# Retention of prompt tiles 3 to 5 moved from the phases before the gathers into the second group's front

## The chip, the cores and the metric

One of the eight cores of a Trainium2 chip runs the whole program. The metric is the device time of one execution in microseconds. The kernel before ran three times: 3722.57, 3725.55 and 3727.93 us, median 3725.55 us.

## The reference

One layer works on 1024 prompt tokens (8 tiles of 128) and 128 sample tokens (one tile, number 8), width 1024, float32 throughout.

```
h = rms_norm(x);  z = h @ w_in         # split into rq rk rv rg (retention), fq fk fv (attention), ff
retention:  rotary on rq, rk; state recurrence over the tiles; output o = intra part + q @ state
            state' = state * decay + k^T v      (tile t needs the state after tile t-1)
attention:  QK-normed, with a cumulative forget bias, causal over all earlier tiles
x = x + concat(rms(o) * silu(rg), rms(attention)) @ w_out
x = x + peer(rms_norm(x)):  q = x @ wq; scores against 2 x 128 keys per head, top 16 of each side,
            16 best of the sums -> 128 experts per token (8 heads x 16);
            y += sum over the 128 experts of softmax * gelu(x . u[e]) * v[e]
```

Every token takes 128 rows of the table `peer_uv` (u and v side by side, 8 KB each). That is 1152 gathers of 128 rows, 1208 MB, for nine tiles.

## The kernel before, in words

**Phases ahead of the tail.** Four programs run one after the other with a barrier between (line 105): `phase_norm` (normed rows turned into `hT`, and the RQ projection), `projection([RK, RV])`, `phase_retention` (recurrence, gate projection RG, gated output stored to `rets`; the sample's new state in four pieces, one in each of four steps; the loads and stores on SP), and `projection([FQ, FK, FV])` for tiles 0 to 2. The list `EARLY` says which tiles the retention half does here: all but `AFTER = [6, 7]`, so tiles 0 to 5 and 8. In all these phases the normed rows of tiles 3 to 8 are also stored to the scratch `hts`, and the pair state after tile 5 to `bds`.

**The tail.** `phase_tail` has two kinds of work on the same engines. The *strips*: for each tile 128 gathers by POOL (L1842) into a ring of nine buffers, a dot product of each on DVE (L2748), four at a time weighed into a strip (L2757 to L2770, with a tanh on ACT, L2055), and added on PE (L2391), which frees four buffers. There are 32 strips to a tile. The *front*: attention, output projection, query projection, scores and top-k choice of the tiles that come later, in three groups of three tiles. A choice ends with ACT moving 16 blocks of indices (L1894); tile t's first gathers wait for those moves. So group 1's front has to be done when tile 2's gathers run out, and group 2's when tile 5's do.

**What sets the order.** `front_steps` lists the front's steps with what each needs, `deal` places every step of every engine between two units of strip work (gather, dot, strip) by a table of assumed costs, and the engines then run these fixed lists. A step that finds no place while there is still strip work is put ahead of the next tile's first unit. Within an engine nothing overtakes.

**Steps in the diff and the prediction.** Group 1's front is, in order: `pmm` and the like (FQ, FK, FV of tiles 3 to 8), `decay`/`foxs`/`foxp`/`foxv` (attention), `hturn`/`hmm` (output projection), `rq` (query projection, L2339: 4 blocks x 3 tiles), `rturn` (L2348), `rscore` (L2357), `rtop` (L2441 to L2454), `rcand` (the choice, L2467 to L2539), `rexp` and `rmove` (the index and gate moves). `retain` lists the retention of late tiles: `lload` (weights, 2 MB each), `lhts` (normed rows, rotary tables, pair state), `lmm` (a projection of a tile, L2159), `lrot`/`lcat` (rotary, L2598 to L2607), `lturn`, `lsc`, `lout`, `lup`. Before the change `retain` is called for group 2 alone. The `rcand` of tile 3 needs the last `rscore` of group 1.

Of the kernel before, what the change touches and what calls it, by code (L numbers as in the profile page):

```python
# [32 lines left out]
def emit(nc, a):  # L33

    ctx = ExitStack()
    with ctx:
# [83 lines left out]
        AFTER = [6, 7]  # L120
# [478 lines left out]
        def phase_retention(block, sem, ps):  # L599
# [3 lines left out]
            PIECE = {ORDER[2 + r]: r for r in range(PAIRS)}  # L603
# [35 lines left out]
            def _(sp):  # L639
# [7 lines left out]
                for s, t in enumerate(ORDER):  # L647
                    sp.wait_ge(rg_done, s + 1)
                    sp.dma_start(a["rets"][t], mixo[:, t, 0:GW]).then_inc(out_done, 16)
                    if t in PIECE:  # L650
                        r = PIECE[t]
# [13 lines left out]
            def _(pe):  # L665
# [100 lines left out]
                for s, t in enumerate(ORDER):  # L766
# [14 lines left out]
                    if t in PIECE:  # L781
                        state_sample(PIECE[t])
                    for k in range(LEAD if t == ST else 0 if whole else KC - 1, KC):
                        gate(t, k)
                    if t == ST:
                        turn_sample()
# [14 lines left out]
            def _(dve):  # L801
# [66 lines left out]
                for s, t in enumerate(ORDER):  # L868
                    if s + 1 < STEPS:
                        mask(ORDER[s + 1])  # L870
                    if t < PT:
                        state(t)
                    if t in PIECE:
                        add_state(PIECE[t])
                    if s + 1 < STEPS and ORDER[s + 1] in PIECE:
                        spread(PIECE[ORDER[s + 1]])
                    gated(t)

# [54 lines left out]
        LATE, NL = TILES - GT, len(AFTER)  # L933
# [6 lines left out]
        def front_steps():  # L940
# [49 lines left out]
            def retain(g, routed):  # L990

                n, NJ = 4 * GT, 4 * NL
                add(rest, ("lload", g, 0), sp=(bulk((2.1, 16)), ("pe", ("rq", g - 1, 2 * GT - 1, 1))))
                add(rest, ("lload", g, 1), sp=(bulk((2.1, 16)), ("pe", ("rq", g - 1, 3 * GT - 1, 1))))
                add(rest, ("lhts", g), sp=(bulk((0.52 * NL, 4), (0.1, 0.25), (0.26, 2)), ("pe", ("rq", g - 1, n - 1, 1))))
                for j in range(NJ + 1):
# [16 lines left out]
                    elif m >= 3 * NL:  # L1013
                        add(rest, ("lgate", g, m), act=(0.7, ("pe", ("lmm", g, m, 1))),
                            dve=(2.0, ("act", ("lgate", g, m)), ("pe", ("lmm", g, NJ - 1, 1))))
# [63 lines left out]
            for g in range(GROUPS):  # L1079
                lo, hi, nt = FIRST[g], FIRST[g + 1], len(tiles_of(g))  # L1080
                routed = [("pe", ("rscore", g - 1, 4 * GT - 1))] if g else []
                if g == 1:
                    project(routed + [("dve", ("rtop", 0, 4 * GT - 1, 4))])
                    routed = [("sp", ("pact", 0, PJ - 1)), ("sp", ("pturn", 0, 2 * LATE - 1)), ("sp", ("pnrm", 0, 2 * LATE - 1))]
                if nt < GT:
                    retain(g, routed)
                    routed = [("dve", ("lret", g, NL - 1)), ("dve", ("lup", g, NL - 1))]
# [19 lines left out]
                if g:  # L1107
                    at = routed if nt < GT else [("sp", ("pturn", 0, 2 * LATE - 1)), ("pe", ("pmm", 0, 2 * LATE - 1, 1))]
                    add(rest, ("loadk", g), sp=(bulk((0.26 * (GT * g + nt), 4)), *at))
# [264 lines left out]
        def phase_tail(block, sem, ps):  # L1374
# [33 lines left out]
            def wq(g, b):  # L1408
# [23 lines left out]
                   for i in range(LATE)]  # L1432
# [5 lines left out]
            NL = len(AFTER)  # L1438
            l_h = [M[:, 35840 + D * i:35840 + D * (i + 1)].rearrange("p (k n) -> p k n", k=KC) for i in range(NL)]
            l_rot = [M[:, 34304 + GW * i:34304 + GW * (i + 1)] for i in range(3)]  # L1440
            l_q = [M[:, 37888 + GW * i:37888 + GW * (i + 1)] for i in range(NL)]
            l_qT, l_kT = ([S[:, o + GW * i:o + GW * (i + 1)].rearrange("p (r n) -> p r n", r=PAIRS) for i in range(NL)]
                          for o in (0, 1024))
            l_kn, l_v, l_g = ([S[:, o + GW * i:o + GW * (i + 1)] for i in range(NL)] for o in (2048, 7944, 8968))
            l_turn = l_g[1][:, 0:3 * NL * 32].rearrange("p (a t d) -> p a t d", a=3, t=NL)
            l_bd = S[:, 9992:10504].rearrange("p (r e) -> p r e", r=PAIRS)
            l_sum = spare[:, GW + D:GW + D + PAIRS * HD].rearrange("p (r e) -> p r e", r=PAIRS)
            l_e = [M[:, W0 + GW * i:W0 + GW * (i + 1)] for i in range(NL)]
            l_sT = [M[:, W0 + 1024 * (1 + i):W0 + 1024 * (2 + i)].rearrange("p (q r l) -> p q r l", q=2, r=PAIRS)
                    for i in range(NL)]  # L1450
            l_gain = M[:, W0 + 3072:W0 + 3584]
            l_o, l_sq, l_w = ([M[:, W0 + o + GW * i:W0 + o + GW * (i + 1)] for i in range(NL)] for o in (4096, 5120, 6144))
# [66 lines left out]
            lup, lst, lsq, lss, lrs, lret, lst_out = (sem(x) for x in ("lup", "lst", "lsq", "lss", "lrs", "lret", "lst_out"))  # L1519
# [29 lines left out]
            def _(sp):  # L1549
# [29 lines left out]
                def front(step):  # L1579
# [36 lines left out]
                    elif kind == "lload":  # L1616
                        q = arg[0]
                        if q < 2:
                            sp.wait_ge(q_mm, 4 * GT * (g - 1) + GT * (q + 2))
                        else:  # L1620
                            sp.wait_ge(lz, NL * (q - 1))
                        sp.dma_start(pw[q % 2], a["c_win"][:, RQ + q]).then_inc(lw_in[q % 2], 16)
                    elif kind == "lhts":
                        sp.wait_ge(q_mm, 4 * GT * g)
                        for i, t in enumerate(AFTER):
                            sp.dma_start(l_h[i].rearrange("p k n -> p (k n)"), a["hts"][t]).then_inc(lh_in, 16)
                        for i, name in enumerate(("c_cos", "c_nsin", "c_psin")):
                            sp.dma_start(l_turn[:, i], a[name][:, AFTER[0]:AFTER[-1] + 1, :]).then_inc(lt_in, 16)
                        sp.dma_start(l_bd, a["bds"].rearrange("p (r e) -> p r e", r=PAIRS)).then_inc(lb_in, 16)
                    elif kind == "lgain":  # L1630
                        sp.wait_ge(lz, 3 * NL)
                        sp.dma_start(l_gain, a["ret_out_g"].rearrange("a h d -> a (h d)").partition_broadcast(P)
                                     .rearrange("p a c -> p (a c)")).then_inc(lg_in, 16)
                    elif kind == "lup":
                        sp.wait_ge(lst, NL)
                        for par in range(2):
# [3 lines left out]
                    elif kind == "loadk":  # L1640
                        w = (tiles_of(g)[-1] + 1) * P
                        sp.wait_ge(s_mm, 4 * GT * g)
                        if g == 1:
                            sp.wait_ge(pz, 2 * LATE)
                            sp.wait_ge(pt_out[0], 16 * LATE)
                            sp.wait_ge(pt_out[1], 16 * LATE)
# [3 lines left out]
                    elif kind == "load":  # L1650
                        t0, n = GT * g, len(tiles_of(g))
                        if g:
                            sp.wait_ge(s_mm, 4 * GT * g)
                        if g == 1:
                            sp.wait_ge(pz, PJ)
# [5 lines left out]
                        if g == 1:  # L1661
                            load_v(range(t0))
                            sp.wait_ge(pk_out[0], 8 * LATE)
# [1240 lines left out]
```

## Time and profile before

| | |
|---|---|
| three runs, median | 3725.55 us |
| profiled execution, its span | 3730.6 us (5 us over the median; it was not timed apart from that) |
| first gather issued | 543.5 us |
| gathers | 1152, first issue to last 543.5 to 3711.3 us |
| gathers' bytes | 1208.03 MB of 1350.24 MB |
| PE / DVE / POOL busy | 63% / 66% / 38% |

The span has two parts. Up to some 580 us the phases and the first group's front run, PE is busy nine tenths of most slices, and DMA is not. From there on the DMA rate stands near 415 GB/s in nearly every slice of 93 us, while no compute engine is full. A share of DMA of 1.0 means that all 16 DMA engines were moving data.

### The profile page before, as it was taken

The page shows a single profiled execution, that of the slowest core. Times are in us where ns is not written, and L with a number is a line of the kernel's source. Part 1 is how long each engine was busy: PE and PEld are TensorE (multiplying, and loading weights), DVE is VectorE, ACT ScalarE, POOL GpSimd, SP SyncE. Part 2 cuts the span into 40 slices and gives each one's busy share as a digit, 9 for nine tenths or more (in the row PEclk, how much of TensorE's full clock was granted, in tenths as well). Part 3 has the DMA queues.
Part 4 walks back from the last instruction along what each step waited for, and adds up shares of the span by engine and source line. Part 5 has one row for each costly group of instructions (what it writes and reads, how often), then busy time and mean ns, then how long its engine had stood idle before and what let it go on. Part 6 is the DMA issues. An engine that isn't in the chain of part 4 may idle for free.

```text
span 3730.6 us, 32224 instructions
## 1 busy us (share of the span) xinstructions
PE 2358.7 (63%) x10549; PEld 927.0 (25%) x10549; DVE 2458.9 (66%) x6363; ACT 492.7 (13%) x1368; POOL 1431.5 (38%) x1276
## 2 busy tenths in 40 slices
PE   7999888886666777763765767774343343334333
PEld 4454443332233233220332332331000000000000
DVE  3263247888666578888855665788887565565655
ACT  2011321112222111011201221110111000000000
POOL 1011003563445343444333444344444444444443
PEclk9999899898788899876666788986565656566656
DMA  3024528999999999999999999999999999999999
GB/s 142 2 52 139 195 89 350 391 396 418 413 415 419 421 397 413 413 387 397 417 388 402 404 415 411 405 410 413 418 409 417 418 418 418 415 420 420 419 419 372
DMA packets 226726, 1350.24 MB, mean 362 GB/s; under 512 B 33840, under 2 KB 53176, under 8 KB 75904
## 3 DMA queue, kind: packets, MB, share of 16 engines
q0 software_dynamic: 165888, 1208.03, 78.6%
q1 hardware_dynamic: 60384, 139.57, 10.2%
q8 instruction: 84, 1.38, 0.1%
q14 instruction: 82, 0.67, 0.0%
q10 hardware_dynamic: 288, 0.59, 0.0%
HBM read 1322.73 MB, written 25.37 MB: 361 GB/s over the span
## 4 chain that ended last, share of the span: by engine, by line
DMA 34%; PE 21%; DVE 17%; POOL 9%; issue 7%; ACT 1%; POOLq 0%; DVEq 0%; ACTq 0%
DMA M<-in_peer_uv,M 34%; PE yp L2391 12%; POOL M L1842 8%; DVE M L2748 7%; PE ab L2339 2%; PE d L2138 1%; PE ab L2103 1%; DVE exg L2765 1%; DVE strips L2770 1%; PE ef L2373 1%; DVE M L2446 1%; DVE M L2531 1%; DVE M L2527 1%; PE d L2318 1%; PE c L2318 1%
## 5 line engine op out<-in xcount | busy, mean ns | idle before, releaser
L1842 POOL DMA_INDIRECT M<-in_peer_uv,M x1152 | 1326.8, 1152 | 1767.9 <-PE yp L2391 1429.6
L2748 DVE SCALAR_TENSOR_TENSOR M<-M 128x1024 f32<-128x1024 f32 x1152 | 1408.6, 1225 | 770.7 <-DMA M<-in_peer_uv,M 737.7
L2391 PE MATMUL yp<-M,strips 128*32 128x512 f32 x4608 | 878.5, 903 | 1129.5 <-DVE strips L2770 1087.8
L2391 PEld LDWEIGHTS yp<-M,strips 128*32 128x32 f32 x4608 | 157.3, 144 | 1720.2 <-DVE strips L2770 1331.2
L2055 ACT ACTIVATE gel<-gel 128x4 f32<-128x4 f32 x288 | 59.1, 205 | 1968.7 <-DVE gel L2759 1947.6
L2339 PE MATMUL ab<-M 128*128 128x512 f32 x576 | 263.8, 607 | 5.3 <-ACT M L2009 5.3
L433 PE MATMUL z<-M 128*128 128x512 f32 x368 | 162.2, 597 | 0.9 <-PEq L105 0.9
L2339 PEld LDWEIGHTS ab<-M 128*128 128x128 f32 x576 | 108.3, 195 | 143.6 <-issue 137.9
L2217 PE MATMUL ab<-M 128*128 128x512 f32 x288 | 135.6, 624 | 10.9 <-DVEq L2557 10.9
L2770 DVE SCALAR_TENSOR_TENSOR strips<-gel,exg 128x128 f32<-128x128 f32 x288 | 84.0, 292 | 31.8 <-ACT gel L2055 22.4
L2576 DVE CUSTOM_DVE_ANT_0 M<-ab,M 128x896 f32<-128x896 f32 (+6 forms) x64 | 48.4, 756 | 85.5 <-PE ab L2104 70.7
L2126 PE MATMUL c<-ident,M 128*128 128x128 f32 x288 | 55.8, 308 | 64.9 <-ACT M L1880 58.6
L2748 DVE DVE_READ_ACCUMULATOR M<-M 128x1 f32 x1152 | 95.0, 82 | 0.0
L2103 PE MATMUL ab<-M 64*128 64x512 f32 (+3 forms) x192 | 87.9, 568 | 6.9 <-DVE mins L2576 6.7
L2138 PE MATMUL d<-M 128*64 128x128 f32 x576 | 91.1, 312 | 1.3 <-ACT M L1888 1.3
L2765 DVE TENSOR_TENSOR exg<-e,gel 128x128 f32<-128x128 f32 x288 | 84.1, 292 | 10.0
L433 PEld LDWEIGHTS z<-M 128*128 128x128 f32 x368 | 69.4, 192 | 83.0 <-issue 82.9
L2217 PEld LDWEIGHTS ab<-M 128*128 128x128 f32 x288 | 56.1, 201 | 94.0 <-issue 94.0
L2138 PEld LDWEIGHTS d<-M 128*64 128x64 f32 x576 | 73.4, 157 | 19.3 <-issue 17.2
L2373 PE MATMUL ef<-M,ident 128*32 128x512 f32 x576 | 75.3, 655 | 2.9 <-ACT M L2051 2.4
L1867 ACT ACTIVATE M<-M,mins 128x896 f32<-128x896 f32 (+6 forms) x64 | 49.6, 775 | 186.5 <-DVE mins L2576 184.1
L2159 PE MATMUL ab<-M 128*128 128x512 f32 x128 | 61.7, 632 | 9.0 <-DVEq L2602 9.0
(309 smaller groups left out, 2575.1 us busy)
## 6 DMA issues: line engine op xcount, KB each, us to landing
M<-in_c_win SPq DMA_DIRECT2D x13, 2048.0 KB, 10.3
M<-in_c_wq SPq DMA_DIRECT2D x12, 2048.0 KB, 11.4
M<-in_peer_uv,M POOLq DMA_INDIRECT x1152
M<-in_w_out SPq DMA_DIRECT2D x24, 512.0 KB, 8.0
M<-in_x_prompt SPq DMA_DIRECT2D x16, 512.0 KB, 11.6
x_scratch<-M SPq DMA_DIRECT2D x9, 512.0 KB, 7.9
M<-x_scratch SPq DMA_DIRECT2D x9, 512.0 KB
M<-hts_scratch SPq DMA_DIRECT2D x8, 512.0 KB, 13.0
```

Of the source, the lines that this page charges most:

```text
L433: last = nc.tensor.matmul(z[n % 3][:, :], hT[:, k, t * P:(t + 1) * P], wbuf[:, slot(gi), k, :], start=(k == 0), stop=(k == KC - 1))
L1842: nc.gpsimd.indirect_dma_start(ring[n % NR], None, a["peer_uv"], bass.IndirectOffsetOnAxis(ap=idxH[:, t % 6, s // 4, s % 4:s % 4 + 1], axis=0)
L2103: nc.tensor.matmul(s[:, c:c + w], rows_q[b0:b0 + 64, r], rows_k[b0:b0 + 64, r, c:c + w], start=True, stop=c + w < width)
L2138: last = nc.tensor.matmul(Dk[b0:b0 + 64, 0:P], (vg if g else vn)[:, j, h * HD:(h + 1) * HD], pT[:, n % 2, j, :], start=(j == 0), stop=(j = ...
L2217: last = nc.tensor.matmul(half_ab[j % 2], hTl[i][:, k, :], pw[q % 2][:, k, :], start=(k == 0), stop=(k == KC - 1))
L2318: last = nc.tensor.matmul(out_bank(t, c), mixed(t)[:, k, :], wout(g, k)[:, 512 * c:512 * c + 512], start=(k == 0), stop=(k == KC - 1))
L2339: last = nc.tensor.matmul(half_ab[i % 2], xT[:, tt, k, :], wq(g, b)[:, k, :], start=(k == 0), stop=(k == KC - 1))
L2373: last = nc.tensor.matmul(EF[32 * b:32 * b + 32, half, :], ident[:, 32 * j:32 * j + 32], xb[:, 512 * half:512 * half + 512], start=True, s ...
L2391: last = nc.tensor.matmul(yp[32 * j:32 * j + 32, 512 * c:512 * c + 512], strips[:, n % 2, j, :], ring[(4 * n + j) % NR][:, D + 512 * c:D + ...
L2748: nc.vector.scalar_tensor_tensor(out=row, in0=row, scalar=1.0, in1=xrep[:, s % 4, :], op0=ALU.mult, op1=ALU.mult, accum_out=dots[:, t % 2, ...
L2765: link(nc.vector.tensor_tensor(exg[:, :, :], bc(e32[:, :].unsqueeze(1), [P, 4, 32]), bc(g[:, 3, :].unsqueeze(2), [P, 4, 32]), ALU.mult))
L2770: nc.vector.scalar_tensor_tensor(out=strips[:, n % 2], in0=bc(g[:, 2, :].unsqueeze(2), [P, 4, 32]), scalar=1.0, in1=exg[:, :, :], op0=ALU. ...
```

## The change

`RETAINED = {1: [3, 4, 5], 2: [6, 7]}` takes the place of `AFTER`. The phases ahead of the tail do the retention half of tiles 0, 1, 2 and 8 only, and `retain` is called for group 1 as well, after that group's FQ, FK, FV projections and before its attention; it loads the normed rows of tiles 3 to 5 and the pair state after tile 2, and leaves its outputs in `mix` and the new pair state in `bds`, where group 2's `retain` finds it. The sample state's four pieces now go two to a step. Buffers, semaphore counts and loads follow.

```diff
-        AFTER = [6, 7]
+        RETAINED = {1: [3, 4, 5], 2: [6, 7]}
+        AFTER = [t for late in RETAINED.values() for t in late]
...
-            PIECE = {ORDER[2 + r]: r for r in range(PAIRS)}
+            PIECE = {ORDER[2]: (0, 1), ORDER[3]: (2, 3)}
...
                     if t in PIECE:
-                        add_state(PIECE[t])
-                    if s + 1 < STEPS and ORDER[s + 1] in PIECE:
-                        spread(PIECE[ORDER[s + 1]])
+                        add_state(PIECE[t][0])
+                        spread(PIECE[t][1])
+                    elif s + 1 < STEPS and ORDER[s + 1] in PIECE:
+                        spread(PIECE[ORDER[s + 1]][0])
                     gated(t)
+                    if t in PIECE:
+                        add_state(PIECE[t][1])
+                        if s + 1 < STEPS:
+                            spread(PIECE[ORDER[s + 1]][0])
...
+                if g == 1:
+                    before = [("pe", ("pmm", 0, PJ - 1, 1)), ("pe", ("pmm", 0, 2 * LATE - 1, 1))]
+                    clear = [*routed, ("act", ("rmove", 0, GT - 1))]
...
-                if nt < GT:
-                    retain(g, routed)
-                    routed = [("dve", ("lret", g, NL - 1)), ("dve", ("lup", g, NL - 1))]
+                if g in RETAINED:
+                    retain(g, routed)
+                    last = len(RETAINED[g]) - 1
+                    routed = [("dve", ("lret", g, last)), ("dve", ("lup", g, last))]
+                if nt < GT:
                     add(rest, ("sload", g), sp=(bulk((0.5, 0.5), (0.6, 2), (2.1, 4)), *routed))
...
                     elif kind == "lup":
-                        sp.wait_ge(lst, NL)
-                        for par in range(2):
+                        sp.wait_ge(lst, NKEPT[g] + len(RETAINED[g]))
+                        if g == 1:
+                            sp.dma_start(a["bds"].rearrange("p (r e) -> p r e", r=PAIRS), l_bd).then_inc(lbd_out, 16)
+                        for par in range(2) if g == 2 else ():
...
-                            i0 = NL if n < GT else 0
-                            sp.dma_start(mix[:, i0:, 0:GW], a["rets"][t0 + i0:t0 + GT].rearrange("t p c -> p t c")
-                                         ).then_inc(mix_in, 16)
+                            i0 = len(RETAINED[g])
+                            if i0 < GT:
+                                sp.dma_start(mix[:, i0:, 0:GW], a["rets"][t0 + i0:t0 + GT].rearrange("t p c -> p t c")
+                                             ).then_inc(mix_in, 16)
```

The lists that `deal` makes change at three places that matter here. (Line numbers of the changed kernel are some 40 higher.)

PE before the change, the end of tile 2 and the start of tile 3. `yp<-M,strips` is a strip, `ef<-M,ident` and `yp<-M,ident` prepare the next tile, `ab<-M 64x64` and `ab<-M 128x64` are retention steps of group 2:

```order
L2391 MATMUL yp<-M,strips 32x512 x8
L2203 MATMUL ab<-M 64x64 x8
L2188 MATMUL ab<-M 128x64 x8
L2195 MATMUL ab<-M 128x128 x4
L2391 MATMUL yp<-M,strips 32x512 x8
L2203 MATMUL ab<-M 64x64 x8
L2373 MATMUL ef<-M,ident 32x512 x24
L2391 MATMUL yp<-M,strips 32x512 x8
L2385 MATMUL yp<-M,ident 32x512 x8
L2391 MATMUL yp<-M,strips 32x512 x48
```

PE after the change, the same place. L2379 is `rq`, L2388 `rturn`, L2397 `rscore`; between the last strip of tile 2 and `yp<-M,ident` of tile 3 (L2425, further down) stand four and a half query blocks with their turns and scores (those shown and three more), and then group 2's first retention steps (L2199):

```order
L2413 MATMUL ef<-M,ident 32x512 x24
L2431 MATMUL yp<-M,strips 32x512 x8
L2379 MATMUL ab<-M 128x512 x4
L2388 MATMUL c<-ident,M 128x128 x4
L2397 MATMUL d<-M 128x128 x4
L2379 MATMUL ab<-M 128x512 x8
```

Group 1's queries stood 17 strips ahead of that place before, and now reach over it.

DVE before the change, the end of tile 3's choice (L2527, L2531, L2534, L2537, L2539) with dot products (L2748) between:

```order
L2748 SCALAR_TENSOR_TENSOR M,dots<-M 128x1024
L2527 TENSOR_TENSOR M<-M,iota 128x1024
L2748 SCALAR_TENSOR_TENSOR M,dots<-M 128x1024
L2531 TENSOR_TENSOR M<-M 128x1024
L2748 SCALAR_TENSOR_TENSOR M,dots<-M 128x1024
...
L2534 TENSOR_REDUCE M<-M 128x64
L2537 SCALAR_TENSOR_TENSOR M<-M 128x128
L2539 TENSOR_TENSOR M<-M 128x128
```

DVE after the change, the same choice (L2567, L2571, L2574, L2577, L2579):

```order
L2567 TENSOR_TENSOR M<-M,iota 128x1024
L2638 TENSOR_TENSOR M<-ab,M 128x512
L2639 TENSOR_TENSOR M<-ab,M 128x8x32
L2640 TENSOR_TENSOR M<-ab,M 128x8x32
L2645 TENSOR_TENSOR M<-M 128x512
L2649 TENSOR_TENSOR M<-M,dec 128x512
L2571 TENSOR_TENSOR M<-M 128x1024
L2574 TENSOR_REDUCE M<-M 128x64
L2577 SCALAR_TENSOR_TENSOR M<-M 128x128
L2579 TENSOR_TENSOR M<-M 128x128
```

No dot product stands between its parts any more, nor ahead of it back to the top-k of the sixth query block; rotary steps of group 2 (L2638 to L2649) do.

SP in the retention phase before: the FQ weights (L658) are loaded one step ahead of the last store of retention outputs (L649).

```order
L649 DMA rets_scratch<-M 128x512
L654 DMA out_new_state_ret_s<-M 64x8x64 x2
L658 DMA M<-in_c_win 128x4096
L649 DMA rets_scratch<-M 128x512
L661 DMA bds_scratch<-M 128x512
L105 UNCONDITIONAL_BRANCH
```

And after: they stand behind the last outputs and behind all pieces of the sample state.

```order
L650 DMA rets_scratch<-M 128x512
L654 DMA out_new_state_ret_s<-M 64x8x64 x4
L658 DMA M<-in_c_win 128x4096
L661 DMA bds_scratch<-M 128x512
L105 UNCONDITIONAL_BRANCH
```

## Rows read from the trace of the kernel before

**Rows 1.** The page: busy time by engine; DMA share and rate in 40 slices
```profile
PE 2358.7 (63%) x10549; PEld 927.0 (25%) x10549; DVE 2458.9 (66%) x6363; ACT 492.7 (13%) x1368; POOL 1431.5 (38%) x1276
...
DMA  3024528999999999999999999999999999999999
GB/s 142 2 52 139 195 89 350 391 396 418 413 415 419 421 397 413 413 387 397 417 388 402 404 415 411 405 410 413 418 409 417 418 418 418 415 420 420 419 419 372
```

**Rows 2.** Windows: busy us (instructions) of each engine; clock, DMA share, GB/s
```profile
900.00:1200.00 300.00, 191.39 (x1091) 86.90 (x1091) 202.77 (x440) 71.32 (x199) 124.66 (x113) 0.82 1.01 416
```

**Rows 3.** Timeline of ACT, end of group 1's routing (start us, us, ...)
```profile
1603.26 4.30 ACT L1894 CAST M<-M 32x32 int32<-32x32 f32 x16
```

**Rows 4.** Timeline of POOL: the first gather of tile 3
```profile
1624.32 1.60 POOL L1842 DMA_INDIRECT M<-in_peer_uv,M  x1 [5.59 <-PE yp L2391]
```

**Rows 5.** Timeline of PE before the tail
```profile
44.08 7.03 PE L297 MATMUL z<-M 128*128 128x512 f32 x16
...
52.26 7.03 PE L297 MATMUL z<-M 128*128 128x512 f32 x16
...
109.90 7.03 PE L433 MATMUL z<-M 128*128 128x512 f32 x16
...
117.21 7.03 PE L433 MATMUL z<-M 128*128 128x512 f32 x16
...
154.23 34.50 PE L433 MATMUL z<-M 128*128 128x512 f32 x80
```

**Rows 6.** Timeline of DVE in the first phase
```profile
27.56 0.69 DVE L245 TENSOR_TENSOR M<-z,M 128x512 f32<-128x512 f32 x1 [7.92 <-PE z L297]
...
29.78 0.69 DVE L254 TENSOR_TENSOR M<-M,dec 128x512 f32<-128x512 f32 x1
...
38.07 1.28 DVE L235 SCALAR_TENSOR_TENSOR M<-M,small 128x1024 f32<-128x1024 f32 x1
39.26 0.68 DVE L265 COPY M<-tp 128x512 f32<-128x512 f32 x1
```

**Rows 7.** Timeline of PE in and after the retention phase
```profile
243.57 1.16 PE L673 MATMUL sc<-M 64*128 64x128 f32 x16
...
256.76 1.16 PE L673 MATMUL sc<-M 64*128 64x128 f32 x16
...
293.94 13.90 PE L796 MATMUL sc<-M,ffw 128*8 128x512 f32 x32
...
310.97 20.87 PE L433 MATMUL z<-M 128*128 128x512 f32 x48
```

**Rows 8.** Timeline of DVE: one piece of the sample state
```profile
242.73 0.69 DVE L845 TENSOR_TENSOR M<-opT,M 128x512 f32<-128x512 f32 x1 [0.38 <-PE opT L741]
...
243.86 1.28 DVE L839 TENSOR_TENSOR M<-M,bind 128x512 f32<-128x512 f32 x2
```

**Rows 9.** Timeline of SP: the load of the FQ weights
```profile
294.50 0.34 SPq L658 DMA_DIRECT2D M<-in_c_win  x1
```

**Rows 10.** DMA issues to 620 us: times, KB each, median us to landing
```profile
M<-in_c_win SPq DMA_DIRECT2D x6, 2048.0 KB, 8.4
```

**Rows 11.** Timeline of PE: group 1's queries with a strip between
```profile
1353.05 7.13 PE L2339 MATMUL ab<-M 128*128 128x512 f32 x16
...
1362.17 1.92 PE L2391 MATMUL yp<-M,strips 128*32 128x512 f32 x16
...
1365.03 7.03 PE L2339 MATMUL ab<-M 128*128 128x512 f32 x16
```

**Rows 12.** Chain of waits: one block's tops on DVE
```profile
513.33 0.88 DVE M L2441 x4
...
518.12 1.08 DVE M L2454 x4
```

**Rows 13.** Lines of DVE, 1480 to 1600 us: first and last of 26
```profile
L2531 DVE TENSOR_TENSOR M<-M 128x1024 f32<-128x1024 f32 x4 | 4.9, 1220 | 0.0
...
L2516 DVE TENSOR_SCALAR M<-M 128x128 f32<-128x128 f32 x1 | 0.2, 220 | 0.0
```

More of the change, by code:

```diff
@@ L932, in emit @@
         PAIRED = 84
-        LATE, NL = TILES - GT, len(AFTER)
+        LATE = TILES - GT
+        NKEPT = {g: sum(len(RETAINED[x]) for x in RETAINED if x < g) for g in RETAINED}
         PJ = 3 * LATE
@@ L990, in retain @@
             def retain(g, routed):
+                NL = len(RETAINED[g])
                 n, NJ = 4 * GT, 4 * NL
-                add(rest, ("lload", g, 0), sp=(bulk((2.1, 16)), ("pe", ("rq", g - 1, 2 * GT - 1, 1))))
-                add(rest, ("lload", g, 1), sp=(bulk((2.1, 16)), ("pe", ("rq", g - 1, 3 * GT - 1, 1))))
-                add(rest, ("lhts", g), sp=(bulk((0.52 * NL, 4), (0.1, 0.25), (0.26, 2)), ("pe", ("rq", g - 1, n - 1, 1))))
+                if g == 1:
+                    before = [("pe", ("pmm", 0, PJ - 1, 1)), ("pe", ("pmm", 0, 2 * LATE - 1, 1))]
+                    clear = [*routed, ("act", ("rmove", 0, GT - 1))]
+                else:
+                    before = [("pe", ("rq", g - 1, 2 * GT - 1, 1)), ("pe", ("rq", g - 1, 3 * GT - 1, 1))]
+                    clear = [("pe", ("rq", g - 1, n - 1, 1))]
+                add(rest, ("lload", g, 0), sp=(bulk((2.1, 16)), before[0]))
+                add(rest, ("lload", g, 1), sp=(bulk((2.1, 16)), before[1]))
+                add(rest, ("lhts", g), sp=(bulk((0.52 * NL, 4), (0.1, 0.25), (0.26, 2)), *clear))
                 for j in range(NJ + 1):
@@ L1107, in front_steps @@
                 if g:
-                    at = routed if nt < GT else [("sp", ("pturn", 0, 2 * LATE - 1)), ("pe", ("pmm", 0, 2 * LATE - 1, 1))]
-                    add(rest, ("loadk", g), sp=(bulk((0.26 * (GT * g + nt), 4)), *at))
+                    add(rest, ("loadk", g), sp=(bulk((0.26 * (GT * g + nt), 4)), *routed))
                 add(rest, ("load", g), sp=(bulk((1.6, 2), (0.26 * (GT * g + nt), 2)) if g else bulk((0.4, 2)), *routed))
@@ L1449, in phase_tail, with rows_at, pairs_at @@
[L1449 to L1452, printed above, removed]
+            def rows_at(base, o, n):
+                return [base[:, o + GW * i:o + GW * (i + 1)] for i in range(n)]
+            def pairs_at(base, o, n):
+                return [x.rearrange("p (r n) -> p r n", r=PAIRS) for x in rows_at(base, o, n)]
@@ new lines, in phase_tail @@
+            l_e = {g: rows_at(M, W0, len(RETAINED[g])) for g in RETAINED}
+            l_sT = {1: [scores_at(o) for o in (W0 + 2048, W0 + 3072, 34304)], 2: [scores_at(o) for o in (W0 + 1024, W0 + 2048)]}
+            l_gain = {1: M[:, W0 + 1536:W0 + 2048], 2: M[:, W0 + 3072:W0 + 3584]}
+            l_o, l_sq = {1: rows_at(M, W0 + 4096, 3), 2: rows_at(M, W0 + 4096, 2)}, {1: rows_at(M, W0 + 5632, 3), 2: rows_at(M, W0 + 5120, 2)}
+            l_w = {1: rows_at(S, 7168, 1) * 3, 2: rows_at(M, W0 + 6144, 2)}
@@ L2145, in front @@
                         j, half = arg
+                        kept, NL = NKEPT[g], len(RETAINED[g])
                         q, i = divmod(j, NL)
@@ L2622, in front @@
                     elif kind == "lsc":
                         i = arg[0]
-                        dve.wait_ge(lsc, i + 1)
+                        dve.wait_ge(lsc, NKEPT[g] + i + 1)
                         for half in range(2):
-                            nc.vector.tensor_tensor(l_sT[i][:, half], four((C, Dk)[half]),
+                            nc.vector.tensor_tensor(l_sT[g][i][:, half], four((C, Dk)[half]),
                                                     bc(causal[:, 0, :].unsqueeze(1), [P, 4, P]), ALU.mult).then_inc(lmask, 1)
```

228 lines of the change are left out of this document (122 added, 106 removed).

## The prediction, made before the changed kernel ran

> **What bounds the kernel now.** I read the page first [rows 1]. PE, DVE and POOL are busy 63%, 66% and 38%, so none of them fills the span, but the DMA row stands at 9 from the ninth slice on. I then took windows inside that part [rows 2]: in 300 us the DMA share is 1.01 at 416 GB/s, with DVE busy 203 and PE 191 of 300. From about 580 us to the end the kernel is bound by bytes: one more MB costs 1000/416 = 2.4 us, and work of PE or DVE costs nothing while it is done before somebody waits for it. Ahead of 580 us PE sets the pace. A change that takes PE work from the first part and puts it beside the gathers is paid for in two ways, by the bytes it adds and by what it does to the deadline of the front. That deadline I read from two timelines. The index moves of tile 3 begin at 1603.3 us [rows 3], and the first gather of tile 3 is issued at 1624.3 us, released by a strip and not by the moves [rows 4]. So the front of group 1 is ready 21 us before it is needed, and no more.
>
> **Removed ahead of the gathers: first phase.** With its query projection a tile takes 52.26 - 44.08 = 8.2 us on PE [rows 5]. Without it the tile goes at the pace of DVE's scaling and copy, 1.28 + 0.68 us [rows 6], about 2.1 with the hand-over. Three tiles give 3 x 6.1 = 18 us. Tiles 6 and 7 lose their wait for a late rotation, and the first tile behind the last query gains one; I take 18.5, between 16 and 21.
>
> **RK and RV.** An RK projection goes at 117.21 - 109.90 = 7.31 us, an RV at 34.50/5 = 6.90 [rows 5]. Three of each are gone: 21.9 + 20.7 = 42.6 us, all of it on PE, which never waits there. Bounds 41 to 44.
>
> **Retention phase.** A step takes 256.76 - 243.57 = 13.2 us [rows 7] and three go: 39.6. The four pieces of the sample's state stay and now sit two to a step. A piece costs DVE 245.1 - 242.7 = 2.4 us [rows 8] (with its spread) and PE 1.1. DVE has under 1 us free in a step, so I give back 2 x 2.4 = 5 us: 34.6. Then comes a new wait. The FQ load is issued at 294.5 [rows 9], under the 15.8 us of forget-gate matmuls (13.9 of them at 293.94), and the next phase's first matmul starts at 310.97 without waiting [rows 7]. After the change the load stands behind the last gated output and the last two pieces on SP. DVE ends its last step 301.5 - 293.9 = 7.6 us behind PE's [rows 7, 8], the two pieces in it add 3.5, the stores 3, then the weights take 8.4 us to land [rows 10], and the store of the pair state behind them is waited for at the barrier. That is 25 us after PE's last step where the matmuls and the barrier cover 17 to 19. I charge 6.5 us, between 2 and 11. The phase gains 28 us, between 24 and 33.
>
> **Sum ahead of the gathers:** 18.5 + 42.6 + 28 = 89 us, between 81 and 98. The last phase and group 0's front are the same instructions.
>
> **Added beside the gathers: bytes.** Four weight blocks of 2.10 MB (8.4), three normed tiles (1.57), rotary tables, gain and pair state (0.7), less the retention outputs no longer read back (0.79): 9.9 to 10.1 MB. At 416 GB/s [rows 2] this is 24 us, between 20 and 28. Nothing hides it, because the DMA engines are full.
>
> **Added: the front's deadline.** Twelve projections of 6.9 us, six rotations, three scores, outputs and updates go ahead of group 1's attention. In the order of PE its attention begins 22 strips later and its queries 24 strips later, while there were 17 strips and 21 us free at the end. The lists show what is left: at the end of tile 2 four and a half query blocks, their turns and scores, six blocks of tops and the whole choice of tile 3 stand behind the last strip of tile 2 and ahead of anything of tile 3. POOL has no indices and DMA runs dry. I count from the landing of tile 2's last gather:
> - its dot product, weighing and strip: 5 us, an estimate of which 1.9 us are the strip's matmuls [rows 11].
> - a query block with turn, score and their evacuations takes 1365.03 - 1353.05 - 1.92 = 10.1 us [rows 11]. Half a block with a whole turn and 4 more: 47 us.
> - the last block's evacuation 0.7 and tops 519.2 - 513.3 = 5.9 us [rows 12]. The earlier tops (6 us each) hide under PE's 10.
> - the choice of tile 3, nothing between its parts: the 26 groups of operations that lie between the two rows of [rows 13], with the last reduction and two closing operations, sum to 30 us busy; the first piece runs earlier, so 29.
> - three rotations of group 2 that stand inside the choice, 30.5 - 27.6 = 2.9 us each for the same five operations [rows 6]: 9 us.
> - exponent, the first four of 16 moves at 4.30/16 us [rows 3], issue and first bytes: 3 us.
>
> Together 99 us without gathers. In that time group 2's loads still run: three weight blocks, two normed tiles and the tables, 7.7 MB, which at 2.4 us per MB take 18 us off the time that follows. Net 81 us. Bounds: if DVE and PE overlap better and the rotations cost half, 65; if a load or a bank makes PE wait between group 2's first projections and the rotations inside the choice, 100.
>
> The Trainium skill speaks against the count of PE. "TensorE: Matmul & The Clock Gate", HAM oscillation, says that repeated idle gaps drop the clock and the work after them runs cold. In the stall PE has a gap of 0.7 us after each query block. By that rule the 47 us could become some 75, and the time 3770. This trace doesn't agree: the blocks of [rows 11] have the same gaps and still take 7.03 us, the time of a block in the first phases [rows 5], that is the upper of the two levels (2.4 GHz), so the sum goes without it.
>
> **Sum.** -89 + 24 + 81 = +16 us. The profiled execution before has a span of 3730.6 us, 5 us over the median of the three runs, so it would become 3747; against the median I predict 3725.6 + 16 = 3742 us. The idle stretch and the bytes together take back 105 us where the phases give 89.
>
> **Rivals.**
> 1. The front still fits (faster). The mechanism: no gather ever waits for tile 3's indices, since PE and DVE have a third of their time free beside the gathers [rows 2] and DMA alone sets the time. Then -89 + 24 = -65, 3661 us. It decides at one point, whether the first gather of tile 3 is released by a strip or by the index moves. For it speaks the free time; against it the engines' fixed order and the 21 us that were free. Chance 0.05. The Trainium skill's "Perfetto Trace Analysis", Optimization Strategy, says that interleaving regimes with different bound engines may improve performance, and stands on this side.
> 2. The stretch is half as long. The steps that stood between strips run closer than I count and group 2's earlier retention, done inside the stall, removes later dips. Idle 60 to 65, net 45: -89 + 24 + 45 = -20, 3706 us. Chance 0.12.
> 3. The stretch is longer. PE falls to the lower clock between its gaps, where a block's eight matmuls take 13.7 us instead of 6.9 (4.5 x 6.9 = 31 us more), or the retention of tiles 3 to 5, waiting for its weights behind full DMA queues, holds strips back in tiles 1 and 2. With 30 us for either: +46, 3772 us. Chance 0.20.
> 4. The change doesn't save what it says: the phases ahead stay bound by something else (the FQ load, rows of x arriving). If 20 of the 89 us are missing, +36, 3762 us. Against it: PE runs there without a gap in [rows 5]. Chance 0.05, counted with the third.
>
> The forecast holds 0.58 with its own range 3722 to 3765.
>
> **How the numbers follow.** A measurement of this kernel tells 0.2%, 7.5 us, from no change. Slower by more: 0.46 of the forecast's 0.58, and all of rivals 3 and 4, 0.71. Within: 0.10 of the forecast and 0.04 of the second rival, 0.14. Faster: 0.02 of the forecast, 0.08 of the second and 0.05 of the first, 0.15. The range for 8 in 10 leaves out the first rival, a third of the second and the end of the third: 3704 to 3785 us.
>
> **What would show it.** Right: the first gather is issued some 89 us earlier, near 455 us; 384 gathers later POOL has one wait of 80 to 110 us, released by ACT's index moves, with two to four windows of 25 us near 0.2 DMA share; the bytes of the hardware queue rise by 10 MB; everything from tile 3 on keeps its pace. In the retention phase the first matmul of the FQ projection waits for its weights. Each is a term of the sum and can be read apart. Wrong: POOL's wait at gather 384 is under 40 us, or there are dips of the DMA rate in tiles 1 and 2 that the kernel before doesn't have, or the first gather comes later than 465 us.

## The result, and the profile after

The changed kernel takes 3784.0 us, median of 4 runs (3783.0 to 3786.3); the kernel before, run beside it, 3726.7. The ratio is 1.0137 with a 95% interval of 1.0114 to 1.0161: slower by 51 us (42 to 60). The two medians lie 57 us apart, the ratio puts it at 51; both are within that interval. The prediction was 3742, range 3704 to 3785: the sign is right, the size is not, and the time lies at the very end of the range. The profiled executions have spans of 3784.5 and 3730.6 us, +53.9; the terms below are measured on them.

The page of the changed kernel: busy time by engine, then the DMA share, the rate in 40 slices and the bytes.
```profile
PE 2374.4 (63%) x10543; PEld 935.4 (25%) x10543; DVE 2457.6 (65%) x6363; ACT 493.1 (13%) x1368; POOL 1416.0 (37%) x1276
...
DMA  3145289999999999928999999999999999999998
GB/s 141 40 139 193 99 351 386 400 408 403 406 398 373 413 419 417 375 84 315 416 396 414 394 418 404 419 376 414 417 415 410 421 418 417 415 418 422 416 421 369
DMA packets 227766, 1359.56 MB, mean 359 GB/s; under 512 B 34368, under 2 KB 53704, under 8 KB 76432
```
Beside [rows 1] nothing stands out in the busy times. The rate row does: the gathers start a slice earlier, and slice 18, at 84 GB/s, is a hole that the kernel before doesn't have. The bytes went from 1350.24 to 1359.56 MB, +9.3.

Ahead of the gathers, the timeline of PE (answering [rows 5, 7]): start, duration, line and operation, then the idle time before it and what ended that.
```profile
55.68 8.80 PE L298 MATMUL z<-M 128*128 128x512 f32 x16 [0.83 <-ACT M L194]
67.49 0.66 PE L307 MATMUL ztp<-ident,M 128*128 128x128 f32 x4 [3.01 <-DVE M L255]
69.07 3.37 PE L434 MATMUL z<-M 128*128 128x512 f32 x4 [0.93 <-PEq L105]
...
189.24 1.58 PE L741 MATMUL opT<-M 128*64 128x512 f32 x4 [1.05 <-DVE M L841]
...
203.97 1.58 PE L741 MATMUL opT<-M 128*64 128x512 f32 x4 [1.04 <-DVE M L841]
205.48 13.90 PE L798 MATMUL sc<-M,ffw 128*8 128x512 f32 x32
...
225.32 0.69 PE L422 MATMUL ffp<-ident,M 8*128 8x8 f32 x9 [4.19 <-PEq L105]
225.94 6.25 PE L434 MATMUL z<-M 128*128 128x512 f32 x10
```
The forget gate's matmuls start at 205.48 where they started at 293.94 [rows 7], 88.5 us earlier, and the phase behind them at 225.94 instead of 310.97, 85.0 earlier: the wait for the FQ weights (4.19 us in front of L422) is there and takes back 3.4.

The timeline of POOL: the first gather of all, then the last one of tile 2 and the first of tile 3, then the last ones of two groups of four behind the hole.
```profile
454.33 1.21 POOL L1881 DMA_INDIRECT M<-in_peer_uv,M  x1 [15.76 <-ACT M L1933]
...
1586.98 0.94 POOL L1881 DMA_INDIRECT M<-in_peer_uv,M  x1 [0.30 <-issue]
1699.88 1.35 POOL L1881 DMA_INDIRECT M<-in_peer_uv,M  x1 [111.96 <-ACT M L1933]
...
1710.88 0.94 POOL L1881 DMA_INDIRECT M<-in_peer_uv,M  x1 [0.30 <-issue]
1724.85 1.90 POOL L1881 DMA_INDIRECT M<-in_peer_uv,M  x1 [13.02 <-PE yp L2431]
...
1749.51 0.94 POOL L1881 DMA_INDIRECT M<-in_peer_uv,M  x1 [19.04 <-PE yp L2431]
```
The first gather is at 454 us, and at gather 384 POOL waits 112 us, released by ACT's index moves; in [rows 4] the same gather was released by a strip. Behind the hole two more waits of 13 and 19 us follow, and these end with strips.

Windows of 25 us around it: busy us (instructions) of PE, PEld, DVE, ACT and POOL, then clock, DMA share, GB/s.
```profile
1575.00:1600.00 25.00, 19.43 (x80) 8.43 (x80) 16.79 (x59) 4.52 (x10) 5.37 (x5) 0.86 0.96 381
1600.00:1625.00 25.00, 22.04 (x114) 8.89 (x114) 16.44 (x85) 6.62 (x13) 0.00 (x0) 1.00 0.13 43
1625.00:1650.00 25.00, 22.30 (x69) 10.79 (x68) 15.33 (x88) 3.92 (x7) 0.00 (x0) 1.00 0.12 52
1650.00:1675.00 25.00, 20.24 (x49) 8.87 (x47) 20.34 (x123) 1.76 (x3) 0.00 (x0) 0.86 0.16 57
1675.00:1700.00 25.00, 20.42 (x49) 9.40 (x50) 23.90 (x33) 2.12 (x8) 0.12 (x1) 0.86 0.34 126
1700.00:1725.00 25.00, 23.42 (x98) 10.18 (x97) 22.64 (x101) 9.97 (x34) 9.54 (x10) 1.00 0.99 396
1725.00:1750.00 25.00, 16.49 (x72) 9.43 (x70) 24.41 (x31) 2.02 (x4) 5.05 (x5) 0.73 0.59 246
1750.00:1775.00 25.00, 14.21 (x88) 7.82 (x88) 23.22 (x47) 1.63 (x4) 14.65 (x13) 0.59 0.79 303
1775.00:1800.00 25.00, 6.76 (x32) 1.19 (x32) 20.09 (x60) 8.43 (x35) 8.22 (x8) 0.52 1.03 336
```
Four windows are nearly empty of bytes: (43 + 52 + 57 + 126) x 25 us = 7.0 MB, which are group 2's loads. Three more, 1725 to 1800, lack (170 + 113 + 80) x 25/416 = 22 us, while DVE is busy 24.4, 23.2 and 20.1 of 25. The lines of DVE in 1725 to 1775 say with what: count | busy, mean ns.
```profile
L2792 DVE SCALAR_TENSOR_TENSOR M<-M 128x1024 f32<-128x1024 f32 x14 | 17.1, 1220 | 0.2
L2658 DVE RECIPROCAL M<-M 128x512 f32<-128x512 f32 x2 | 6.7, 3353 | 0.1
L2571 DVE TENSOR_TENSOR M<-M 128x1024 f32<-128x1024 f32 x3 | 3.7, 1230 | 0.0
```
Only 14 dot products (L2792) in 50 us; between them stand the gates of group 2's retention (the reciprocals) and tile 4's choice (L2571), which the order put behind the first strips of tile 3.

**Equal bytes.** To add the terms up I summed the rate column of 25 us windows over each span and read when the same number of MB had been moved. The figures are this time less that of the kernel before; a column's steps show where time is lost or won. Each column is one profiled execution, so single steps are good to a few us. A column's level ahead of the gathers is worth less: the change, e3 to e7, e9 and e12 all have tiles 3 to 5 late, and their first gathers are issued between 448.0 and 462.2 us.

| MB moved (before: at us) | change | e1 | e2 | e3 | e4 | e5 | e6 | e7 | e8 | e9 | e10 | e11 | e12 |
|---|---|---|---|---|---|---|---|---|---|---|---|---|---|
| 75 (616) | -87 | -39 | -31 | -90 | -92 | -79 | -92 | -81 | 0 | -93 | -57 | -32 | -91 |
| 175 (866), in tile 0 | -87 | -39 | -32 | -72 | -92 | -79 | -92 | -80 | 20 | -79 | -61 | -34 | -91 |
| 475 (1592), near the end of tile 2 | -71 | -32 | -26 | -37 | -79 | -63 | -81 | -23 | 65 | -44 | -42 | -7 | -84 |
| 575 (1842), in tile 3 | 27 | 19 | 3 | -15 | 19 | 21 | 19 | -5 | 63 | -25 | -13 | 4 | 15 |
| 1325 (3660) | 32 | 16 | -5 | -14 | 22 | 22 | 26 | -11 | 47 | -29 | 7 | 1 | 23 |

So the change is -87 (phases), +16 (tiles 1 and 2), +98 (around gather 384), +5 (later), and +22 for 9.3 MB more at 416 GB/s: +54, against +53.9 of the spans.

### The profile page after: what moved, and what is told of

It is laid out like the page before. It is cut to its first block, busy times and chain, and to the rows that moved or that the text cites. A ratio compares the mean times of both kernels' runs of the same rounds, so it can differ in the third digit from the quotient of the medians.

```text
span 3784.5 us, 32186 instructions
## 1 busy us (share of the span) xinstructions
PE 2374.4 (63%) x10543; PEld 935.4 (25%) x10543; DVE 2457.6 (65%) x6363; ACT 493.1 (13%) x1368; POOL 1416.0 (37%) x1276
## 2 busy tenths in 40 slices
DMA packets 227766, 1359.56 MB, mean 359 GB/s; under 512 B 34368, under 2 KB 53704, under 8 KB 76432
## 4 chain that ended last, share of the span: by engine, by line
DMA 36%; PE 24%; DVE 17%; POOL 8%; issue 6%; ACT 1%; POOLq 0%; DVEq 0%; ACTq 0%
DMA M<-in_peer_uv,M 35%; PE yp L2431 12%; POOL M L1881 7%; DVE M L2792 7%; PE ab L2379 2%; PE ab L2142 1%; PE ef L2413 1%; DVE exg L2809 1%; PE d L2358 1%; DVE strips L2814 1%; PE d L2177 1%; PE ab L2199 1%; DMA qts_scratch<-M 1%; PE ab L2257 1%; DVE M L2486 1%
## 5 line engine op out<-in xcount | busy, mean ns | idle before, releaser
L1881 POOL DMA_INDIRECT M<-in_peer_uv,M x1152 | 1309.0, 1136 | 1899.6 <-PE yp L2431 1450.0
L2792 DVE SCALAR_TENSOR_TENSOR M<-M 128x1024 f32<-128x1024 f32 x1152 | 1407.2, 1225 | 814.7 <-DMA M<-in_peer_uv,M 781.4
L2379 PE MATMUL ab<-M 128*128 128x512 f32 x576 | 263.7, 607 | 5.3 <-ACT M L2048 5.3
L2199 PE MATMUL ab<-M 128*128 128x512 f32 x320 | 153.0, 632 | 11.4 <-issue 6.5
L2379 PEld LDWEIGHTS ab<-M 128*128 128x128 f32 x576 | 108.1, 195 | 140.1 <-issue 134.4
L2257 PE MATMUL ab<-M 128*128 128x512 f32 x288 | 135.7, 625 | 10.7 <-DVEq L2597 10.7
L434 PE MATMUL z<-M 128*128 128x512 f32 x272 | 122.3, 607 | 0.9 <-PEq L105 0.9
L2792 DVE DVE_READ_ACCUMULATOR M<-M 128x1 f32 x1152 | 94.5, 82 | 0.0
L2199 PEld LDWEIGHTS ab<-M 128*128 128x128 f32 x320 | 62.9, 203 | 98.8 <-issue 97.0
L2257 PEld LDWEIGHTS ab<-M 128*128 128x128 f32 x288 | 56.1, 201 | 94.0 <-issue 94.0
```

The lines of the kernel that those rows point to most:

```text
L434: last = nc.tensor.matmul(z[n % 3][:, :], hT[:, k, t * P:(t + 1) * P], wbuf[:, slot(gi), k, :], start=(k == 0), stop=(k == KC - 1))
L1881: nc.gpsimd.indirect_dma_start(ring[n % NR], None, a["peer_uv"], bass.IndirectOffsetOnAxis(ap=idxH[:, t % 6, s // 4, s % 4:s % 4 + 1], axis=0)
L2199: last = nc.tensor.matmul(half_ab[j % 2], l_h[i][:, k, :], pw[q % 2][:, k, :], start=(k == 0), stop=(k == KC - 1))
L2257: last = nc.tensor.matmul(half_ab[j % 2], hTl[i][:, k, :], pw[q % 2][:, k, :], start=(k == 0), stop=(k == KC - 1))
L2379: last = nc.tensor.matmul(half_ab[i % 2], xT[:, tt, k, :], wq(g, b)[:, k, :], start=(k == 0), stop=(k == KC - 1))
L2792: nc.vector.scalar_tensor_tensor(out=row, in0=row, scalar=1.0, in1=xrep[:, s % 4, :], op0=ALU.mult, op1=ALU.mult, accum_out=dots[:, t % 2, ...
```

## The experiments

Theory A: the loss is the front's deadline, the hole that the order of the steps leaves ahead of tile 3. Its rival, theory B: the loss is contention (bytes, held strips, clock) and goes with the amount of work beside the gathers. Ratios are against the kernel before on the same chip; in us they are taken of 3727.

**e1 and e2: fewer late tiles.**
```diff
-        RETAINED = {1: [3, 4, 5], 2: [6, 7]}
+        RETAINED = {1: [4, 5], 2: [6, 7]}      # e2: {1: [5], 2: [6, 7]}
```
(with the retention outputs of the other tiles of group 1 read back, as before.)

> Only tiles 4 and 5 (with 6 and 7) are late; tile 3 keeps its retention ahead of the gathers. Theory A, the deadline of the front sets the loss: the phases ahead save about 62 us (two thirds of 18 + 43, and two steps of the retention phase less the pieces), the bytes cost 22, and in DVE's order 45 steps instead of 70 stand ahead of the first dot product of tile 3, so POOL's wait at gather 384 is about 60 us instead of 112 and costs 45 to 55 net. Sum about +15, 3740 us. Theory B, the loss is contention (bytes, dips in tiles 1 and 2, low clock) and grows with the number of late tiles: two thirds of what the change shows, +36, 3762 us, and the wait stays above 90 us.

> Only tile 5 (with 6 and 7) is late. Theory A: the phases ahead save 29 us, the bytes cost 21, 21 steps instead of 70 stand ahead of the first dot product of tile 3: POOL's wait at gather 384 is about 35 us, 28 net. Sum about +20, 3745 us, no less than with two tiles. Theory B: one third of the change's loss, +18, 3744 us, with dips in tiles 1 and 2 instead of a wait at gather 384. The two differ in the wait, not in the time.

Measured: e1 1.0050 (1.0028 to 1.0072), +19 us; e2 1.0046 (1.0021 to 1.0072), +17. The waits of POOL from 1500 to 1850 us: total, times, longest, first in e1, then in e2.
```profile
POOL M L1880 <- ACT M L1932: 62.6, 3, 62.0
```
```profile
POOL M L1880 <- ACT M L1932: 39.1, 3, 38.5
```
With 70, 45 and 21 steps of DVE ahead of tile 3's first dot product (in the traces some 330, 170 and 50 instructions between the last dot product of tile 2 and that one) the wait is 112, 62 and 38.5 us, where theory A said 60 and 35. It falls with what the order leaves behind the last strip of tile 2, while the bytes stay the same (1359.5 MB in both). Theory B fails on e1: its wait of 90 us isn't there. On the times, e1 (+19) lies near A's +15 and far from B's +36; e2 (+17) fits both, as was said ahead of it.

**e3: let the front go ahead of strips; e8: the same in the kernel before.**
```diff
-                        if start + cost <= bound + slack[e]:
+                        wide = {"pe": 9, "dve": 6}.get(e, slack[e]) if did["pe"] < 96 else slack[e]
+                        if start + cost <= bound + wide:
```

> Tiles 3 to 5 late as in the change, but in tiles 0 to 2 the order lets a step of the front go ahead of a strip when it delays it by up to 9 us on PE and 6 us on DVE (2.5 before); the front of group 1 is then through ahead of tile 3 in the order. Theory A: the wait at gather 384 falls from 112 us to under 25; the phases' 86 us stay, bytes 22, dips of the DMA rate in tiles 0 to 2 grow from 16 to 30 or 40 us because the ring of buffers takes up most delays of 9 us. Sum -86 + 22 + 35 + 10 = about -20, 3706 us. Theory B: what is not idle in one place is idle in another, the sum of dips and wait stays near 115 us and the time at +50, 3776 us.

> Control: the kernel before with the wide slack (9 us on PE, 6 on DVE) in tiles 0 to 2 and no other change. Its front was through 21 us before it was needed, so nothing is to be gained there. Theory A: strips held back in tiles 0 and 1 cost as in the run with the wide slack, 25 to 45 us: 3760 us. If the wider order is simply better, it is faster than before by about the 8 us that the wide run showed, and then the change itself gave nothing in that run.

Measured: e3 0.9978 (0.9962 to 0.9994), -8 us, the only version below the kernel before whose interval leaves out 1; e8 1.0133 (1.0092 to 1.0175), +50. In e3 no wait is left that ACT's moves end; the waits of POOL there are, in the same stretch:
```profile
POOL M L1882 <- PE yp L2432: 183.4, 26, 16.1
POOL M L1882 <- issue: 25.0, 82, 0.3
```
The hole is gone and 59 us of time with it (1.0137 to 0.9978), but not for nothing: tiles 0 to 2 lose 52 us (16 in the change) and tile 3 another 23. The control shows the price of the order by itself: 65 us lost in tiles 0 to 2, 18 won back behind them. So e3 is faster because of the change and in spite of its order. Theory A holds; its price for the held strips, 30 to 40 us, was too low.

**e4: fewer bytes.** The four blocks are loaded to a quarter.
```diff
+                        kk = 2 if g == 1 else KC
-                        sp.dma_start(pw[q % 2], a["c_win"][:, RQ + q]).then_inc(lw_in[q % 2], 16)
+                        sp.dma_start(pw[q % 2][:, 0:kk], a["c_win"][:, RQ + q, 0:kk]).then_inc(lw_in[q % 2], 16)
```

> The change, but the four weight blocks of the retention of tiles 3 to 5 are loaded to a quarter (two of eight parts; the projections use what stood in the buffers), 6.3 MB less. If the bytes beside the gathers are paid for at the DMA's rate, 15 us less than the change: +39, 3765 us. If they are hidden in dips and in the wait at gather 384, no difference: +54. A part of the dips in tile 1 may go too, if they came from the loads: then under +30.

Measured: 1.0096 (1.0076 to 1.0117), +36: 15 us less than the change for 6.3 MB, which agrees with the price of 2.4 us per MB. The two intervals together leave 4 to 27, so "hidden" is out, but the price itself isn't measured any closer than that; the wait at gather 384 stayed at 112.4 us. In the table tiles 1 and 2 lose 13 us where the change loses 16: a quarter of the weights to load leaves most of those dips.

**e5: group 2's rotations behind tile 3's choice.**
```diff
+                        late += [("act", ("rexp", 1, 0))] if m == 0 and g == 2 else []
```

> The change, but the rotations of group 2's retention may not start before the exponent of tile 3's choice, so the three that stood inside the choice stand behind it. The prediction charged 9 us for them (2.9 each). Theory A, everything between the last strip of tile 2 and tile 3's indices is on the path: POOL's wait at gather 384 goes from 112 us to 103, the time to +45 us, 3771, or less gain if group 2's front, now 6 strips later in the order, brings dips of its own in tiles 3 to 5. Theory B, DVE isn't what ends the wait (PE or ACT is): the wait stays at 112.

Measured: 1.0087 (1.0056 to 1.0119), +32, where I forecast +45. The wait, from 1500 to 1800 us:
```profile
POOL M L1882 <- ACT M L1934: 103.7, 3, 103.1
```
112.0 - 103.1 = 8.9 us for three rotations, where [rows 6] gave 3 x 2.9 = 8.7. By the table another 5 us are won in tile 3 and 4 later (98 to 84, then 5 to 1). A likely reason is that gates and scores move with the rotations out of the first strips of tile 3; that was not tried by itself.

**e6 and e12: thinner work with the same order.** In e6 each of the twelve projections does 2 of its 8 matmuls, in e12 DVE's rotation products and gates are done for one head of eight.
```diff
+                        for k in ((0, 7)[half],) if g == 1 else range(4 * half, 4 * half + 4):
```
```diff
+                        nh = 1 if g == 1 else NH
...
+                        w = HD if g == 1 else GW
...
+                        dl(nc.vector.reciprocal(l_w[g][i][:, 0:w], l_e[g][i][:, 0:w]))
```

> The change, but each of the twelve projections of tiles 3 to 5 beside the gathers does 2 of its 8 matmuls (work left out); all waits, loads, DVE and ACT operations stay, in the same order. Theory A: the wait at gather 384 is set by what stands behind the last strip of tile 2 in the order and stays at 112 us. If the dips of tiles 1 and 2 (16 us in the change) come from PE holding strips back behind projections, they fall by about 8, and the time is +46, 3772 us. If they come from the weight blocks on the DMA queues or from DVE, nothing changes: +54. Theory B, PE's total work sets the loss: 12 x 5.2 = 62 us less PE work makes the wait shorter by tens of us.

> The change, but in the retention of tiles 3 to 5 DVE's products of the six rotations and the three gates are done for one head of eight (work left out), 19 us less DVE work with the same steps, waits, loads and PE work. The wait at gather 384 stays at 112 us. If the 16 us of dips in tiles 1 and 2 come from DVE holding dot products back behind such steps (a reciprocal of 3.35 us), they fall to 8 or less: +46, 3772 us; if from the low clock of PE or its order, they stay: +54.

Measured: e6 1.0130 (1.0082 to 1.0179), +48; e12 1.0110 (1.0065 to 1.0155), +41; their intervals overlap with the change's, so the times tell neither from it. The waits that ACT's moves end, in e6 and in e12:
```profile
POOL M L1881 <- ACT M L1933: 112.5, 3, 111.9
```
```profile
POOL M L1881 <- ACT M L1933: 112.6, 3, 112.0
```
The longest wait at gather 384 is 111.9 us in e6 and 112.0 in e12: 12 x 5.2 = 62 us less PE work changes it by 0.1 us. In the table tiles 0 to 2 lose 11 us in e6 and 7 in e12, where the change loses 16. That points to DVE's long steps for about half of the dips and to PE's for some. One profile each, with steps good to a few us, doesn't show the split.

**e7, e9: the slack elsewhere, and both moves.** e7 widens tiles 1 and 2 alone, by 12 us on PE; e9 is e3 with e5.
```diff
+                        wide = {"pe": 12, "dve": 6}.get(e, slack[e]) if 32 <= did["pe"] < 96 else slack[e]
```

> As the run with the wide slack, but tile 0 keeps the order of the change, and in tiles 1 and 2 PE's steps may delay a strip by up to 12 us (DVE 6). In that run 17 of the 52 us of dips lay in tile 0. Theory A: the 86 us of the phases stay through tile 0; dips in tiles 1 and 2 30 to 35 us, around the boundary to tile 3 20, bytes 22: about -12, 3714 us. Theory B, a sum that is preserved: what isn't lost in tile 0 is lost at the boundary, about 0, 3727 us.

> Both moves together: the wide slack in tiles 0 to 2 (9 us on PE, 6 on DVE) and group 2's rotations behind the exponent of tile 3's choice. The wide run alone was at -8 us against before, the rotations alone gave the change 18 us back, 9 of them in the wait at gather 384 and the rest in the strips behind it. Theory A, the two act on different places (tiles 0 to 2, and the boundary to tile 3 with what follows): -8 minus about 10, -18, 3709 us. Theory B, both only fight the same wait, which the wide slack has removed already: no more than -8, and less if group 2's front, 9 strips later, brings dips in tiles 3 to 5.

Measured: e7 1.0037 (1.0015 to 1.0060), +14, where I forecast -12: tile 0 keeps its 80 us as said, but tiles 1 and 2 lose 57 instead of 30 to 35. The preserved sum (+0) is nearer than my -12, and the time is above both. e9 0.9990 (0.9943 to 1.0037), where I forecast -18: its four runs tell it neither from the kernel before nor from e3, though its profiled execution has the shortest span of all, 3724.0.

**e10, e11: two and one late tile with both moves**, the slack 5 us on PE and 4 on DVE in e10, 6 and 4 in e11.

> Only tiles 4 and 5 late, a mild slack (5 us on PE, 4 on DVE) in tiles 0 to 2, and group 2's rotations behind tile 3's choice. By the terms so far: phases -62, bytes +22, dips from the slack about 12, wait at gather 384 with 24 steps ahead of it in DVE's order instead of 45, about 35 us and 25 net: -3, 3724 us. If the wait costs less than its length, because group 2's loads run in it, -10.

> Only tile 5 late, slack of 6 us on PE and 4 on DVE in tiles 0 to 2, rotations behind tile 3's choice. By the terms: phases -29, bytes +21, dips from the slack about 15, no wait of more than 20 us at gather 384, 5 net: +12, 3739 us. It tells whether the fixed 8.4 MB of weights make one late tile not worth its bytes even where no wait is left; if the order alone is what counts, it is at -5.

Measured: e11 1.0042 (0.9996 to 1.0088), +16, where I forecast +12. No wait that ACT's moves end is left at gather 384, and still nothing is won: one late tile doesn't earn its 9.2 MB. Its four runs don't tell it from the kernel before. e10 1.0058 (1.0010 to 1.0107), +22, where I forecast -3. Its wait was 42.1 us instead of 35, and 20 us went in the rows of the table from tile 3 to tile 8, where e1 loses nothing. In DVE's order tile 6's choice now ends behind all 768 dot products of the tiles before it (behind 727 in the change), and the trace shows group 2's front at its own deadline, POOL at gather 768:
```profile
2775.29 0.94 POOL L1882 DMA_INDIRECT M<-in_peer_uv,M  x1 [15.92 <-ACT M L1934]
```
In e1, in e11 and in the change no gather from 1900 us on waits for ACT's moves. So most of the 20 us is this second wait.

## Why the prediction was right in sign and too small

- **Phases ahead: right,** the third at the low end of its 24 to 33. The three phases gave -18.1, -42.6 and -24.3 where I had 18.5, 42.6 and 28. These are 85.0; the first load of group 0's routing comes 89.2 us earlier (439.1 for 528.3), for the predicted 89, so that 4 us came in the front of group 0, whose instructions are the same. Within the third phase the FQ wait cost 3.4 us, not 6.5; two pieces to a step make 14.7 us of 13.2 (189.24 to 203.97), and the first two steps got 5 us longer, which the sum didn't have. (The 301.5 us of DVE's last step is the end of this row of the kernel before, which was not shown:)
```profile
300.81 0.69 DVE L863 TENSOR_TENSOR M<-M,small 128x512 f32<-128x512 f32 x1
```
- **Bytes: right.** 9.3 MB and 22 us in all for 10 MB and 24. The count of 10 was for the bytes beside the gathers and holds there: the phases ahead store four retention outputs of 0.26 MB instead of seven, 0.8 MB less, so 10.1 MB more move behind them. In the table these 0.8 MB, 2 us, stand in the -87 of the first row, where the first gather is 89 us earlier. e4 agrees with the price within 4 to 27 us for 6.3 MB.
- **The hole at gather 384: right.** The four query blocks in it stand 10.03 us apart, as counted; three rotations cost 8.9 us. The four windows from 1600 to 1700 moved 7.0 MB, nearly all of it group 2's loads, which is 17 us of traffic (I had 18), and so cost 100 - 17 = 83 us, for 81 net. Rival 1, that the front still fits, is out, and so is rival 2.
- **The step that failed:** "everything from tile 3 on keeps its pace", and with it the sum's silence on tiles 1 and 2. Two terms were missing. Around gather 384 the table has 98 us; 98 - 83 = 15 us are lost behind the hole, while DVE is busy 24.4 of 25 with front steps between its dot products. (The windows behind the hole lack 22 us; the kernel before lacks some 10 at the same place, with 316 GB/s from 1650 to 1675 and 363 from 1700 to 1725, so about this much is new.) That DVE's queue is the cause is read from the lines above; e5, which moves part of it away, gives 5 us back there. And in tiles 1 and 2 the retention's steps hold strips back, 16 us. The second was the latter half of rival 3, to which I gave 30 us and a chance of 0.20, though not by its cause: it had the steps wait for weights behind full DMA queues, and e4, with a quarter of the weights, still loses 13; the test I named for it, dips of the rate in tiles 1 and 2 that the kernel before doesn't have, came out:
```profile
1150.00:1175.00 25.00, 18.47 (x98) 8.98 (x90) 15.05 (x33) 5.54 (x15) 13.44 (x12) 0.83 0.86 350
...
1200.00:1225.00 25.00, 17.73 (x95) 7.70 (x98) 13.06 (x31) 3.77 (x10) 8.93 (x8) 0.70 0.81 322
```
In [rows 2] the rate over 300 us of tile 1 is 416, and in tiles 1 and 2 of the kernel before, up to 1650 us, no window of 25 us is under 377. With 16, 15 and 5 us (later tiles) the sum of +16 becomes +52; the rest are the small errors above.
- **The clock: right.** In the hole PE has a gap of 0.68 us behind each evacuation, a block keeps its 7.03 us, and the clock stands at 1.00 in the two windows from 1600 to 1650, the upper level (2.4 GHz):
```profile
1614.59 7.03 PE L2379 MATMUL ab<-M 128*128 128x512 f32 x16
1622.29 0.65 PE L2388 MATMUL c<-ident,M 128*128 128x128 f32 x4 [0.68 <-ACT M L2054]
...
1624.62 7.03 PE L2379 MATMUL ab<-M 128*128 128x512 f32 x16
```
The section of the Trainium skill that the prediction set against this ("TensorE: Matmul & The Clock Gate", HAM oscillation) describes waits for a DMA that are longer than the matmuls between them. The gaps here are a tenth of the matmuls between them. So the 28 us more that I read out of it stretched the rule beyond its case, and this trace says nothing against the rule itself.

## What to carry to other kernels

Work moved beside a transfer-bound stretch is free only up to two limits, and both are read from the order of the instructions, not from busy shares: how many steps end up behind the last work unit ahead of a deadline (here 70 steps gave 112 us, 45 gave 62, 21 gave 38), and how long a single step may stand in front of a unit that frees a buffer (in the control, steps of PE that may delay a strip by 9 us instead of 2.5 and of DVE by 6 cost 65 us in tiles 0 to 2). Relieving the first limit at the expense of the second moves about half of the loss instead of removing it (e3: 75 us less at the deadline, 36 more ahead of it). Relieving one deadline can also break the next (e10: 16 us at gather 768). After a predicted hole, count the queue that it leaves as well: here it cost another 15 us.

## What the runs showed of the hardware

The clock level of the same code differs from one execution to another. In e1's profile the attention of group 0, ahead of the gathers, ran at the lower level (1.2 GHz) although PE was busy 24.65 of 25 us for two windows:
```profile
350.00:375.00 25.00, 24.65 (x74) 12.30 (x73) 4.12 (x17) 7.97 (x28) 0.00 (x0) 0.50 0.59 209
375.00:400.00 25.00, 24.65 (x75) 12.44 (x74) 3.69 (x16) 8.17 (x28) 0.00 (x0) 0.50 0.03 8
```
In e10, with the same two tiles late, the same stretch has 1.00:
```profile
350.00:375.00 25.00, 22.84 (x122) 12.42 (x120) 6.23 (x28) 12.74 (x46) 0.00 (x0) 1.00 0.74 289
```
From the first scores of group 0's attention to its last product with v, the same instructions took 80 us in e1 and 53 in e10. In both PE was thinly busy just ahead (5.9 of 10 us in e1, 4.3 in e10) and the clock fell below 0.75; in e10 it was back at 1.00 within 20 us, in e1 it stood at 0.50 for the 60 us from 340 to 400. Of these 27 us 18 are left at the first gather (503.1 and 484.8 us), since e10 came into the stretch 9 us later. That is the difference between e1's column, which begins at -39, and e10's, at -57, and about the 17 us by which e1's profiled execution (3770.1 us) lies above its median of 3753.5. A loss in one profile ahead of the gathers is thus to be checked against its clock before it is put down to an edit. That the level stays low under nearly full load for 60 us I had not expected; what holds it there stays open.
